# Tail of a decoder block: half of the last tokens' residual moved from VectorE to ScalarE and two accumulating GpSimd transfers

## The reference, cut to what matters

```
u  = rmsnorm(h, pre_ffn_g)
ff = (silu(u @ w_gate) * (u @ w_up)) @ w_down
h  = h + rmsnorm(ff, post_ffn_g)          # rmsnorm(x, g) = x / sqrt(mean(x*x) + EPS) * g
return h[:, 16:]
```

## Time and profile before

| | |
|---|---|
| median of 3 runs | 1078.55 us (1078.52 to 1079.44) |
| span of the profiled execution | 1076.4 us from the first to the last instruction |
| its own time | not listed apart; the median is 2.15 us more than the span, for what lies around it |
| TensorE busy | 1065.8 us (99%) |
| VectorE, ScalarE, GpSimd busy | 875.0, 589.9 and 27.2 us |
| moved to and from HBM | 202.86 MB read, 4.19 MB written |
| mean granted TensorE clock | 0.998 |

### The profile page before, as it was taken

How to read it: one execution, slowest core, us unless ns; L and a number is a source line. 1 busy time by engine, 2 the same in 40 slices (tenths; PEclk the granted TensorE clock), 3 DMA queues, 4 the chain that set the end, 5 groups by cost and what they waited for, 6 DMA issues and landing times. The chain is left out here.

```text
span 1076.4 us, 15278 instructions
## 1 busy us (share of the span) xinstructions
PE 1065.8 (99%) x5757; PEld 923.4 (86%) x5757; DVE 875.0 (81%) x1113; ACT 589.9 (55%) x724; POOL 27.2 (3%) x46
## 2 busy tenths in 40 slices
PE   9999999999999999999999999999999999999996
PEld 8999999999888888888888888888888888888885
DVE  6699987637646887899899998998998888777787
ACT  6554454736555566565565555655555555554553
POOL 4000001101000000000000000000000000000000
PEclk9999999999999999999999999999999999999999
DMA  8655535444386485665756665666657666656554
GB/s 277 211 177 169 165 117 158 138 137 138 115 298 215 136 276 185 223 195 177 234 179 194 213 194 182 213 186 224 190 182 228 217 202 199 198 195 217 199 198 180
DMA packets 113207, 208.05 MB, mean 193 GB/s; under 512 B 9184, under 2 KB 46496, under 8 KB 111856
## 3 DMA queue, kind: packets, MB, share of 16 engines
q1 hardware_dynamic: 111952, 201.49, 58.9%
q10 hardware_dynamic: 608, 4.20, 0.9%
q0 software_dynamic: 576, 1.40, 0.4%
HBM read 202.86 MB, written 4.19 MB: 192 GB/s over the span
## 5 line engine op out<-in xcount | busy, mean ns | idle before, releaser
L550 ACT ACTIVATE w_hi<-raw 128x1024 fp32r<-128x1024 f32 x326 | 341.6, 1059 | 263.6 <-PE ps L1703 173.1
L903 DVE TENSOR_TENSOR w_lo<-raw,w_hi 128x1024 fp32r<-128x1024 f32 x326 | 395.1, 1227 | 97.2 <-ACT w_hi L550 96.6
L1701 PE MATMUL ps<-w_hi,uf 128*128 128x512 f32 x524 | 205.3, 392 | 0.1
L1703 PE MATMUL ps<-w_hi,uf 128*128 128x512 f32 x524 | 204.1, 389 | 0.0
L1702 PE MATMUL ps<-w_lo,uf 128*128 128x512 f32 x524 | 203.9, 389 | 0.0
L1365 PE MATMUL ps<-u,w_hi 128*128 128x272 f32 (+1 forms) x544 | 158.8, 292 | 0.0
L1367 PE MATMUL ps<-u,w_hi 128*128 128x272 f32 (+1 forms) x544 | 155.9, 287 | 0.0
L1368 PE MATMUL ps<-u,w_lo 128*128 128x272 f32 (+1 forms) x544 | 155.7, 286 | 0.0
L834 ACT CAST t_hi<-tx 128x1024 fp32r<-128x1024 f32 x84 | 87.0, 1048 | 56.0 <-DVE tx L1203 28.6
L1703 PEld LDWEIGHTS ps<-w_hi,uf 128*128 128x128 f32 x524 | 98.4, 188 | 20.7
L1701 PEld LDWEIGHTS ps<-w_hi,uf 128*128 128x128 f32 x524 | 98.4, 188 | 20.4 <-issue 0.5
(11 more groups left out here) (273 smaller groups left out, 1427.1 us busy)
## 6 DMA issues: line engine op xcount, KB each, us to landing
raw<-in_w_gate SPq DMA_DIRECT2D x176, 256.0 KB, 3.0
raw<-in_w_up SPq DMA_DIRECT2D x176, 256.0 KB, 3.6
raw<-in_w_down SPq DMA_DIRECT2D x88, 512.0 KB, 4.1
raw<-in_w_in SPq DMA_DIRECT2D x72, 512.0 KB, 3.6
raw<-in_w_out SPq DMA_DIRECT2D x32, 512.0 KB, 4.6
arena<-in_x SPq DMA_DIRECT2D x2, 1024.0 KB, 6.0
arena<-in_x ACTq DMA_DIRECT2D x2, 1024.0 KB, 9.4
out<-h2rows SPq DMA_DIRECT2D x2, 1024.0 KB, 5.5
```

What stands on the lines that cost most here:

```text
L550: act.activation(w_hi[:, slot, :], raw[:, slot, :], ACT.Copy).then_inc(hi_done, 1)
L903: dve.tensor_tensor(w_lo[:, slot, :], raw[:, slot, :], hi_view(w_hi[:, slot, :]), ALU.subtract).then_inc(lo_done, 1)
L1701: pe.matmul(o, a[0], b[0], start=start, stop=False)
L1703: return pe.matmul(o, a[1], b[0], start=False, stop=stop)
```

## The change

In the last block of tokens (block 1) the first 1024 columns are no longer made by VectorE. Since `h` already lies in those rows of `out`, ScalarE multiplies the two pieces of 512 columns of `f_acc` by `rd` in place (semaphore `tail_scaled`), and GpSimd issues for each a transfer that adds it to what lies in `out` (semaphore `added`). SP's load of `h2rows` for block 1 leaves these columns out, VectorE's `residual(1)` has three pieces in place of four, SP stores three, and at the end SP waits for `added` as well.

```diff
     OUT_PIECES = [[slice(0, D // 2), slice(D // 2, D)],
-                  [slice(0, D // 2), slice(D // 2, 3 * D // 4), slice(3 * D // 4, 7 * D // 8), slice(7 * D // 8, D)]]
+                  [slice(D // 2, 3 * D // 4), slice(3 * D // 4, 7 * D // 8), slice(7 * D // 8, D)]]
+    ADD_PIECES = [slice(0, D // 4), slice(D // 4, D // 2)]
...
+        tail_scaled, added = sem("tail_scaled"), sem("added")
...
             for m in range(NQ):
-                sp_eng.dma_start(h2rows[:, m, :], out_v[:, m, :]).then_inc(h2_back[m], 16)
+                c0 = min(piece.start for piece in OUT_PIECES[m])
+                sp_eng.dma_start(h2rows[:, m, c0:D], out_v[:, m, c0:D]).then_inc(h2_back[m], 16)
...
             sp_eng.wait_ge(stored, 16 * n)
+            sp_eng.wait_ge(added, 16 * len(ADD_PIECES))
...
             pool.tensor_copy(ident_r, ident).then_inc(ident_rounded, 1)
+            pool.wait_ge(h2_kept, 16 * NQ)
+            for k, cols in enumerate(ADD_PIECES):
+                pool.wait_ge(tail_scaled, k + 1)
+                pool.dma_start(out_v[:, NQ - 1, cols], acc_of(NQ - 1, cols), accum_op=ALU.add).then_inc(added, 16)
...
                     inv_rms(rd[:, m:m + 1], sst[:, m:m + 1], D, rd_done)
+            act.wait_ge(rd_done, NQ)
+            act.wait_ge(f_done, len(QUARTERS))
+            for cols in ADD_PIECES:
+                act.activation(acc_of(NQ - 1, cols), acc_of(NQ - 1, cols), ACT.Copy,
+                               scale=rd[:, NQ - 1:NQ]).then_inc(tail_scaled, 1)
```

## The result

The change makes the kernel a little slower: 1080.84 us (1080.23 to 1081.7, 21 runs) against 1079.18 us (1078.52 to 1079.75, 21 runs) of the kernel before, ratio 1.0017 with the 95% interval 1.0011 to 1.0023. That is 1.2 to 2.5 us more. The time lies in the predicted range and the sign is the one forecast, but the forecast difference of 0.55 us is a third of the 1.66 us between the two medians. The base of the forecast, 1078.55 us from three runs, also lay 0.63 us under the median of 21 runs.

A forecast was written before the change was run, and what follows sets the result against it. Only the last 7 us counted: VectorE's residual and SP's stores, nearly level with the 1 MB drain. GpSimd's second transfer, 1071.05 + 4.3 + 1.3 = 1076.65, ends the span at 1077.08, +0.7 on 1078.55: 1079.1 us, range 1077.2 to 1081.5.

The forecast's parts named there:

- the forecast difference of 0.55 us: Whole kernel: predicted 1079.1 us against the base of 1078.55; the sum's +0.7 us was rounded down a little.
- The base of the forecast: Whole kernel before: profiled span of 1076.4 us plus 2.15 us to the median of the runs, carried over unchanged.
- rival A: Tail: GpSimd's second transfer ends last, 5.2 to 6.8 us after its issue; 1078.8 to 1080.5 us; chance 0.46.
- B: Tail: GpSimd's transfers land within 3.7 us, hidden, so SP's stores end last; 1077.35 us; chance 0.17.
- D: Tail: storing 1 MB is the bound, whoever issues it, so nothing shows; 1078.0 to 1078.7 us; chance 0.16.
- On SP's side the gain is 1.20 us, and not more: Tail, VectorE and SP: without the 1024-column piece, VectorE's last piece ends at 1071.40 in place of 1072.60 us.
- the 0.57 us of SP's late issue: Tail: SP's last issue stands 0.57 us behind VectorE's end because the issue before took 0.58 us; kept unchanged.
- the 2.8 us of landing: Tail: SP's last store lands 2.8 us after its issue, as before; issued at 1071.97, landing at 1074.77 us.
- ScalarE's pieces and the way to GpSimd: Tail: copies of about 0.604 us, pieces ready at about 1070.4 and 1071.0, GpSimd's issues at 1070.45 and 1071.05 us.
- Issue to landing: GpSimd's second transfer: 4.3 us, middle of 3.0 and 5.7, plus 1.3 us for the addition; landing at 1076.65 us.
- two source reads: GpSimd's accumulating transfers: by the skill's rule the extra is some 1.5 us in place of the forecast's 1.3.
- C: Tail: engines wait for the old value at each row, landing 7.1 us or more after issue; 1082.4 us; chance 0.19.

## Why the prediction was right, and where its terms were off

What was right is the sign and its reason: GpSimd's second transfer ends last, 6.0 us after its issue, which is rival A. The time of 1080.84 us is 0.34 over A's own range, and the base of that range was 0.63 low. The range as a whole says little for the prediction, since it reached over A, B and D.

VectorE and SP's side: the residual is 1.20 us shorter, as forecast. "On SP's side the gain is 1.20 us, and not more" was wrong. I kept the 0.57 us of SP's late issue and the 2.8 us of landing as if they were fixed, but with half the bytes both shrink: the run with nothing in place of the columns gained 2.2 us in its tail. Nor does the reason given for the 0.57 us account for it: the issue before, of 0.58 us, ended at 1072.82, and the last began only at 1073.17. This was hidden in the changed kernel, whose end SP doesn't set, but it was the floor of rival B and of the range.

ScalarE's pieces and the way to GpSimd: I put `rd` to the second piece at 1.26 us and took 0.05 us for GpSimd's wait, which no row had shown. The copies took 0.72 and 0.71 us, not 0.60; the row that I took was of a copy without a scale, to another type and into another tile, and no run tells which of these counts. GpSimd's record of an issue begins 0.61 us after the end of the copy that releases it, at both issues, and 0.60 to 0.61 after it in the other profiles. The second issue stands 1.98 us behind `inv_rms` where I had 1.31: 0.67 us of the error.

Issue to landing: forecast 4.3 + 1.3 = 5.6 us, measured 6.0, of which 3.9 are what the second plain transfer took and 2.1 the addition. That the sum came so near is in part luck, for the first term was 0.4 too high and the second 0.8 too low. Without the addition GpSimd's transfers land in 3.4 and 3.9 us and a single one in 3.5, near the bound from SP's store; the loads from the start of the kernel stood among full engines and said little of the tail. The addition costs more than 1.3 us: 3.7 us of each engine's time for what plain transfers do in 1.4. I had it as one more reading, which should be a factor of 2. The packets behind the first ones show just that (0.18 against 0.09 us for 2 KB, 0.33 against 0.17 for 4 KB); what the sum lacked are the long first packets, which bring the whole to 2.4 at equal packets and 2.6 as the two kernels have them. I also let part of the reading overlap, and nothing shows that it does.

The rule of the Trainium skill, "Collectives: The Full Stack", in the section on why ReduceScatter is half of AllGather, of two source reads, fits these later packets with their factor of 2, and is too low for the whole transfer. The rule of the Trainium skill, "DMA: Bandwidth & Descriptors", section "Anatomy of one DMA", gives an estimate of 2.6 us for a plain 256 KB; measured 3.5 in the tail from GpSimd's issue, so here it is about 0.9 us short.

From the last landing to the end of the span: 0.43 us before, 1079.3 - 1078.55 = 0.75 after, 0.32 us of the error. No run takes this apart.

Together: 0.67 + 0.4 + 0.32 = 1.39 us, which is the difference between the forecast of 0.68 us (1077.08 - 1076.4) and the 2.07 us in the profile.

The rivals. B, hidden transfers, is out at 6.0 us from issue to landing; not because of GpSimd's queue (3.4 and 3.9 us without the addition, near the 3.7 that B asks for), but for the addition. C, a wait for the old value at every row, is out as the rule (0.04 us a row), though the first packet of an engine does take half a microsecond and more (0.54 us on average with one piece). D, that the drain of the 1 MB is the bound whoever issues it, was given 0.16 and describes the plain transfers well: three versions with 0.5 MB or 0.25 MB on another way (ratios 1.0001, 0.9999, 0.9995) are not told from the kernel before, and their data takes 3.5 to 3.6 us from the first packet to the last as it did before. That is where the expected gain of 1.20 us went even without the addition: some 0.5 us of the earlier first packet is left, which the times don't resolve.

Open is why the first accumulating packets take so long. That accumulating packets delay SP's stores is shown by the pair with and without the addition. The reading of the old value as the cause is argued only, though the factor of 2 a packet fits it.

## What to carry to other kernels

At the end of a kernel count the bytes that still have to leave before counting instructions: taking 1.2 us off the engine on the path brought nothing that could be measured while 1 MB had to be stored behind it. An accumulating transfer is no free addition; at 2.4 to 2.6 times the engine time of a plain one it belongs where nothing waits for the DMA engines. A queue's time read at a busy place is not its time at a quiet one: GpSimd's load of 256 KB took 5.5 us at the start of this kernel, its plain store of 256 KB 3.5 in the tail (no run has the same transfer in both places). And compare profiles from an event just ahead of the change; here the executions differed by up to 1.4 us before the tail began.

## What the runs showed of the hardware that was not expected

- Accumulating transfers to HBM moved 133 to 160 GB/s with all 16 engines full, 3.7 us of each engine's time for 0.5 MB, and 3.4 in packets of 4 KB; plain ones in packets of 4 KB took 1.4 us. Behind the first ones a packet took twice the time of a plain one of its size (0.18 against 0.09 us, 0.33 against 0.17).
- The first 16 accumulating packets took 0.54 us each on average, the later ones 0.18. Beside such a transfer SP's plain stores landed after 4.3 us, beside the plain one after 3.1.
- From the end of ScalarE's instruction to the recorded start of GpSimd's issue 0.61 us passed, and an accumulating issue took 0.96 us where the plain one took 0.58 (the two runs with one piece of 512 columns, accumulating and plain):

```profile
1071.43 0.96 POOL L543 DMA_DIRECT2D out<-f_acc  x1 [818.77 <-ACT f_acc L909]
```

```profile
1071.32 0.58 POOL L543 DMA_DIRECT2D out<-f_acc  x1 [818.77 <-ACT f_acc L909]
```
